# Four weight slots of a two-block transformer kernel, each moved to another place modulo 256 bytes

## The reference

```
proj = h @ w_in                                  # 2048 x 8192
y = einsum('bsgc,gcd->bsgd', pooled, w_group)    # 4 x 1024 x 1024
x = x + (y * silu(gate)) @ w_out                 # 4096 x 2048
...
q = (rmsnorm(q_lat) @ w_q_b); kv = c @ w_kv_b    # latent attention, 16 heads
...
x = x + g1 * (concat(out_a, out_b) @ w_out_2)
u, g = split(h @ w_up)                           # 2048 x 11264
x = x + g2 * ((silu(conv(u)) * g) @ w_down)      # 5632 x 2048
```

## The kernel before

| tiles | address modulo 256, before |
|---|---|
| `w_hi`, `w_lo`, all four slots | 128 |
| `h_hi`, `h_lo`, `f_hi`, `f_lo`, `pool_hi`, `pool_lo`, `y_hi`, `y_lo`, `hk_hi`, `c_hi`, `q_hi` | 64 |
| `y_mid_hi`, `y_mid_lo`, `mixw_hi`, `mixw_lo`, `hk_lo`, `lat_hi` | 192 |
| `raw`, all four slots | 128 |

## Time and profile before

### The profile page before, as it was taken

How to read it: one execution, slowest core, us unless ns; L and a number is a source line. 1 busy time by engine, 2 the same in 40 slices (tenths; PEclk the granted TensorE clock), 3 DMA queues, 4 the chain that set the end, 5 groups by cost and what they waited for, 6 DMA issues and landing times.

```text
span 2078.1 us, 41240 instructions
## 1 busy us (share of the span) xinstructions
PE 2047.4 (99%) x17698; PEld 2017.3 (97%) x17698; DVE 1567.2 (75%) x2256; ACT 1030.4 (50%) x1339; POOL 15.4 (1%) x23
## 2 busy tenths in 40 slices
PE   8999999999999999998999999999999999999998
PEld 7999999999999999998999899999999999999998
DVE  7988788688687888877855687678876766666666
ACT  6444444444445466654457557454444444444444
POOL 1000000000000000000000000000000000000000
PEclk9999999999999999999999999999999999999999
DMA  8897888889685788658653754668876666666663
GB/s 272 291 355 279 290 306 304 272 281 329 217 271 160 237 286 298 218 180 311 224 165 106 195 175 131 209 205 320 307 234 194 192 196 194 191 199 194 194 193 122
DMA packets 248749, 483.01 MB, mean 232 GB/s; under 512 B 26347, under 2 KB 59735, under 8 KB 248311
## 3 DMA queue, kind: packets, MB, share of 16 engines
q1 hardware_dynamic: 247807, 480.16, 70.0%
q0 software_dynamic: 528, 0.15, 0.0%
q10 hardware_dynamic: 232, 0.06, 0.0%
HBM read 478.17 MB, written 8.44 MB: 234 GB/s over the span
## 4 chain that ended last, share of the span: by engine, by line
PE 95%; DMA 2%; DVE 2%; ACT 1%; issue 0%; POOL 0%; SPq 0%; DVEq 0%; ACTq 0%; POOLq 0%
PE acc L1930 89%; PE side L1930 3%; PE sums L1930 2%; DMA mod_raw<-in_w_mod 2%; DVE w_lo L1205 1%; PE sums L2205 1%; DVE mod_raw L1193 0%; DMA vec_rows<-in_b_q_norm_g 0%; PE sums L2013 0%; ACT w_hi L637 0%; POOL vec_rows L611 0%; DVE xT L1335 0%; POOL vec_rows L607 0%; ACT silu_row L732 0%; SPq L451 0%
## 5 line engine op out<-in xcount | busy, mean ns | idle before, releaser
L1205 DVE TENSOR_TENSOR w_lo<-raw,w_hi 128x1024 fp32r<-128x1024 f32 x681 | 830.6, 1229 | 403.2 <-ACT w_hi L637 396.3
L637 ACT ACTIVATE w_hi<-raw 128x1024 fp32r<-128x1024 f32 x681 | 718.7, 1060 | 818.9 <-PE acc L1930 701.0
L1930 PE MATMUL acc<-h_hi,w_hi 128*128 128x256 f32 x3600 | 851.4, 280 | 10.9 <-DVE xT L1335 6.6
L1930 PE MATMUL acc<-h_lo,w_hi 128*128 128x256 f32 x3600 | 843.3, 278 | 0.0
L1930 PEld LDWEIGHTS acc<-h_hi,w_hi 128*128 128x128 f32 x3600 | 677.5, 189 | 21.9 <-issue 14.3
L1930 PEld LDWEIGHTS acc<-h_lo,w_hi 128*128 128x128 f32 x3600 | 677.3, 189 | 0.1
L1930 PE MATMUL acc<-h_hi,w_lo 128*128 128x256 f32 x3600 | 486.8, 278 | 0.3 <-DVE w_lo L1205 0.3
L1930 PEld LDWEIGHTS acc<-h_hi,w_lo 128*128 128x128 f32 x3600 | 446.2, 189 | 0.4 <-DVE w_lo L1205 0.4
L1193 DVE SCALAR_TENSOR_TENSOR mod_raw<-mod_raw,silu_row 128x1024 f32<-128x1024 f32 x192 | 234.1, 1219 | 15.7 <-DMA mod_raw<-in_w_mod 15.6
L1930 PE MATMUL acc<-f_hi,w_hi 128*128 128x256 f32 x704 | 164.4, 277 | 0.0
L1930 PE MATMUL acc<-f_lo,w_hi 128*128 128x256 f32 x704 | 164.2, 276 | 0.0
(11 more groups left out here) (338 smaller groups left out, 2108.2 us busy)
## 6 DMA issues: line engine op xcount, KB each, us to landing
mod_raw<-in_w_mod SPq DMA_DIRECT2D x192, 512.0 KB, 6.4
raw<-in_w_up SPq DMA_DIRECT2D x176, 512.0 KB, 4.4
raw<-in_a_w_in SPq DMA_DIRECT2D x128, 512.0 KB, 5.2
raw<-in_w_down SPq DMA_DIRECT2D x88, 512.0 KB, 4.6
raw<-in_a_w_out SPq DMA_DIRECT2D x64, 512.0 KB, 5.4
raw<-in_w_in SPq DMA_DIRECT2D x52, 512.0 KB, 3.7
raw<-in_b_w_in SPq DMA_DIRECT2D x40, 512.0 KB, 5.2
raw<-in_a_w_group SPq DMA_DIRECT2D x32, 512.0 KB, 5.4
```

Of the source, the lines that this page charges most:

```text
L637: last = act.activation(w_hi[s][:, :], raw[s][:, :], ACT.Copy)
L1205: last = dve.tensor_tensor(w_lo[s][:, :], raw[s][:, :], f32(w_hi[s][:, :]), ALU.subtract)
L1930: return pe.matmul(o, lhsT, rhs, start=start, stop=stop, skip_group_check=True)
```

## The change

The `w_hi` and `w_lo` slots are allocated one by one with an extra distance of 0, 64, 128 and 192 bytes for slots 0 to 3, and the `w_lo` slots begin 256 bytes further on. To make room, `MID` moves from 114880 to 115392, that is by 512 bytes. The slots get the names `w_hi_a` to `w_hi_d`.

```
-LOW, MOD_AT, W_AT, MID, H_AT, FAR = 16512, 73824, 82048, 114880, 148288, 181056
+LOW, MOD_AT, W_AT, MID, H_AT, FAR = 16512, 73824, 82048, 115392, 148288, 181056
+W_PAD = (0, 64, 128, 192)
...
-        ring = home(W_AT, MID)
-        w_hi = [ring(f"w_hi{s}", [P, SLAB], F32R) for s in range(RING)]
-        w_lo = [ring(f"w_lo{s}", [P, SLAB], F32R) for s in range(RING)]
+        def w_slot_at(part, s):
+
+            at = W_AT + part * (16384 + 256) + s * 4096 + W_PAD[s]
+            return home(at, MID)
+
+        w_hi = [w_slot_at(0, s)(f"w_hi_{'abcd'[s]}", [P, SLAB], F32R) for s in range(RING)]
+        w_lo = [w_slot_at(1, s)(f"w_lo_{'abcd'[s]}", [P, SLAB], F32R) for s in range(RING)]
```

## The result

The changed kernel takes 2138.09 us (2137.83 and 2138.35), against 2102.18 before (2078.23 and 2126.14). So the change is slower, and the time lies outside the forecast range of 2074 to 2127 us. It is rival 3, three or four slots slow, some 3 us above the 2135 at which that rival ended. The profiled execution has a span of 2136.5 us, 58.4 more than before.

A forecast was written before the change was run, and what follows sets the result against it. PE's matmul pitch was taken as the bound. From the profiled 2078.1 us, +24.2 for fast stretches becoming half slow, -0.8 for `y_mid` and +0.7 for switching gave 2102 us, range 2074 to 2127.

The forecast's parts named there:

- rival 3: Weight slots: three or four slow, 2114 or 2126 us, up to 2135 if alternation costs on top; chance 0.25.
- What bounds the kernel: Whole kernel: PE is busy 99% of the span, so only the matmul pitch matters, at about 113.33 or 117.8 ns.
- Once it happens without one: Slabs from 1499.81 us: pitch rises to 117.9 ns at 1502.53 us, claimed to happen without a wait of PE.
- The difference modulo 256 as the cause: All matmuls: token minus weight address modulo 256, plus a phase, decides whether a matmul costs 4.45 ns more.
- I take one of b and d as fast and one as slow: Slots b and d (differences -128 and 0): one at 113.33, one at 117.8 ns, making the four-slot mean 115.56 ns.
- The rule that places 128 bytes apart are opposite: Weight slots: of two places 128 bytes apart, one is fast and one slow; used for b and d.
- The upper bound: Long fast stretches: all four slots slow, 3.94% of 1228 us, +48.4 us, giving 2126.5 us.
- So slot a stays fast and slot c becomes slow: Long stretches: slot a (difference -64) stays at the fast level, slot c (+64) goes to the slow one.
- the prediction's own sign of a wrong mechanism: Profile after: `w_hi_a` and `w_hi_c` alike in a stretch without waits would show the mechanism wrong.
- 630 to 1355 us: ... no change: Stretch from 630 to 1355 us: already about half in each level, so no change in time.
- The spread of the kernel before as its phase: Kernel before: its 2126.14 us run, 47.9 above the profiled one, may be all long stretches slow (+48.4).
- Rival 4: Slots in turn break up the slow phase, mixed stretch and `y_mid` fast as well: 2063 to 2072 us; chance 0.07.

The follow-up runs named there:

- e5: Changed kernel with all weight slots back at 128 modulo 256 and the token tiles moved by 64 bytes (difference 0): 2169.45 us.
- e6: Changed kernel with all weight slots alike at 192 modulo 256 and token tiles moved by 64 bytes (difference -64): 2096.40 us.
- e1: Changed kernel with all four slots alike, back at 128 modulo 256 (difference -64): 2120.24 us.
- e4: Changed kernel with all four slots alike at 64 modulo 256 (difference 0): 2169.26 us.
- g6: Changed kernel with slots a and b at 128 modulo 256 (difference -64), c and d at 0 (+64): 2078.36 us.
- e3: Changed kernel with all four slots alike at 0 modulo 256 (difference +64): 2132.01 us.
- i2: Changed kernel with slots a, b at 128 and c, d at 0 modulo 256, token tiles at 192 moved to 64: 2075.22 us.
- g3: Changed kernel with all slots at 128 modulo 256 and token tiles at 192 moved to 64 (nearly all differences -64): 2101.92 us.

## Why the prediction was wrong

- *What bounds the kernel* was right: PE's pitch decides, with two levels before. DVE and ACT kept their durations, and no wait took over. But waits too short to leave PE idle stand where the level changed: *"Once it happens without one"* misread, where the weight load had waited for DVE.
- *The difference modulo 256 as the cause* was right. e5 and e6 show it: 2169.45 us for difference 0 from moved tokens, 2169.26 from moved weights, and the old times where both moved. The pitches of e1 to e4 even give the changed kernel: (113.3 + 118.65 + 117.8 + 120.0)/4 = 117.4 ns, measured 117.5 in the feed-forward part, and 118.6 with -64 in its slow phase, measured 118.5 up to 540 us. Alternation adds next to nothing.
- *"I take one of b and d as fast and one as slow"* is the step that failed. Both are slow in any phase: alone, difference -128 runs at 118.65 and 0 at 120.0 ns. So the mean of the long stretches is 117.5 to 118.5 ns and not 115.56, and the term for them, forecast at +24.2 us, was some +50: 22.8 up to 540 us, 1.7 with `y`, 2.7 and 22.5 behind 1355 us. The rule that places 128 bytes apart are opposite had one observation behind it (`y` and `y_mid`, -64 and +64), and I carried it over to another pair of places. It isn't even a rule for its own pair: in g6 -64 and +64 both run at 113.3 ns, in e1 and e3 both at 117.8.
- *The upper bound* was mis-sized for the same reason. I bounded b and d by the two levels in view. The stretch with weights at two places in turn ran at 117 ns, and it was the only row with difference -128 in it. It deserved more weight than the rule. Rival 3 came within 3 us of the result by adding a cost of the alternation, and that cost is next to nothing; its 2126 us for four slow slots was too low for the same reason as the bound.
- *"So slot a stays fast and slot c becomes slow"*: in the feed-forward part a is at 113.8 ns and c at 117.9 as forecast. In the first 540 us both are slow, a at 117.9 and c at 117.7 ns by slab starts. That is the prediction's own sign of a wrong mechanism, a and c alike in a stretch without waits. What was wrong is that the phase exchanges the levels of -64 and +64: in the slow phase both are slow. That the mean does not depend on the phase held only on this and on the assumption on b and d.
- *"630 to 1355 us: ... no change"* was +8.7 us; its slabs take the differences -128 and 0 too. *`y_mid`*, forecast at -0.8, came out at nothing.
- *The spread of the kernel before as its phase* was right. Its runs beside i2 fall into three heaps: 10 from 2077 to 2086 us, 9 from 2098 to 2107, and 4 from 2120 to 2127. The two long parts, before 540 us and from 1356 us on, each slow or fast, give 0.0393 x 498 = 20, 0.0393 x 690 = 27, or both, 47 us on 2078. The heaps as such are argued from these sums, since the kernel before has a trace of one execution only. Mixed executions are shown for kernels with its difference: e6's (2102 us, 113.3 ns up to 530 us, 117.8 behind 1400 us), g3's the other way round (2098 us, 117.8 ns up to 530 us, 113.4 behind 1530 us), and e1's (2113 us, 113.3 ns, then 117.8 from 333 us).
- *Rival 4*, that slots in turn break up the slow phase, had 0.07 and was half right: they do so where the slots are at -64 and +64. In the change they did not: in its first 540 us the stream stayed slow on all four, and b and d are slow in either phase.
- *The rule of the Trainium skill* ("TensorE: Matmul & The Clock Gate", section "Step-by-step: what each phase is for": loading the next weights doesn't steal read bandwidth from the running matmul) does not hold here, if it means that the place of the weights cannot matter. Four kernels that differ in this distance alone have medians of 2120 (2082 at its fastest), 2132, 2151 and 2169 us.

What stays open: by which mechanism the distance acts (that the two reads meet in the memory was a guess that no run tested), why some differences have two levels, why a late weight load should change the level, and why a step between differences ends the slow phase at one time and not at another. "Phase" is a name for what the runs show, not an explanation.

## What to carry to other kernels

Where PE is the bound and every matmul has its own weight load, look at the pitch from start to start. Several levels with one shape and one clock pointed to addresses here: try the distance between the stationary and the moving tile modulo 256, each value with all slots alike and then the good ones mixed, since +64 alone would have been thrown out. Look at the weight loads for waits, not at PE alone: a late load need not leave PE idle. A wide spread from run to run can itself be such a matter; a design that steps between two good distances took it from 50 to 3 us and the median from 2100 to 2075 us, while the fastest runs differ by 4 us. Do not extend a rule from one pair of places to another without a row, and let the only row at a place outweigh a symmetry.

## What the runs showed of the hardware that I had not expected

For a 128x128 weight load and a 256-column moving tile in fp32r the steady pitch at full granted clock is, by difference modulo 256, 120.0 ns at 0, 118.3 at -32, 113.3 or 117.8 at -64, 118.65 at -96 and -128, 117.8 at +64. Single stretches of 40 us add 117.3 at -96 (a second level), 116.7 at +32 and 120.0 at +96, and +64 reached 113.3 where slabs at -64 lay in between. At -64 the level changed for hundreds of microseconds (e1, from 333 us on) at a weight load that came some 50 ns late.
